# A four-layer network on one core: the second layer's input projections, two heads at a time, as seven half-size products a pair of blocks

## The reference, cut to what matters

```python
def odd_layer(x, norm_g, w_in, b_forget, w_out):
    hn = rmsnorm(x, norm_g)
    proj = hn @ w_in                      # (256, 2048) @ (2048, 4*2048 + 16)
    q, k, v, z, f_logit = jnp.split(proj, cuts, axis=-1)
    log_f = jax.nn.log_sigmoid((f_logit + b_forget).astype(jnp.float32))
    o = forgetting_attention(q, k, v, log_f)   # 16 heads of 128, causal
    o = o * jax.nn.silu(z)
    return x + o @ w_out
```

## Time and profile before

| | |
|---|---|
| median of three runs | 2799.68 us (2799.62 to 2801.92) |
| the profiled execution | 2801.85 us |
| its span, first to last instruction | 2800.0 us |
| mean granted TensorE clock, share of full speed | 0.997 |
| TensorE matmuls / weight loads busy | 2765.9 us (99%) / 2507.3 us (90%) |
| VectorE, ScalarE, GpSimd busy | 1165.1 (42%), 589.1 (21%), 216.8 us (8%) |
| read from HBM | 397.56 MB, 143 GB/s over the span |
| the 16 heads of the second layer | 554.66 to 1026.85 us |
| its output projection, 8 pairs | 1026.85 to 1126.94 us |

### The profile page before, as it was taken

The page is one execution under the profiler, slowest core; times in us unless marked ns, Lnnn a source line. Parts: engine busy times, 40 slices in busy tenths (PEclk is TensorE's granted clock), DMA queues, the critical chain, the costliest instruction groups (busy, mean ns, idle before and its releaser), DMA issues.

```text
span 2800.0 us, 45537 instructions
## 1 busy us (share of the span) xinstructions
PE 2765.9 (99%) x17268; PEld 2507.3 (90%) x17268; DVE 1165.1 (42%) x2805; ACT 589.1 (21%) x1321; POOL 216.8 (8%) x451
## 2 busy tenths in 40 slices
PE   8999999999999999999999999999999999999997
PEld 6888889999999999899999999888889999888897
DVE  6667665500001036544445541111113565444555
ACT  3221211111111112333333320111111012222211
POOL 0111110000000000222222210000000000000000
PEclk9999999999999999999999999999999999999999
DMA  6434433444343435333333326333332444444442
GB/s 233 143 129 148 140 115 135 153 167 148 136 149 136 149 135 194 122 120 123 132 133 123 134 97 228 134 120 120 120 136 79 177 165 162 163 155 150 150 166 105
DMA packets 63259, 400.50 MB, mean 143 GB/s; under 512 B 6705, under 2 KB 13377, under 8 KB 16865
## 3 DMA queue, kind: packets, MB, share of 16 engines
q1 hardware_dynamic: 62976, 397.58, 40.3%
q0 software_dynamic: 224, 2.11, 0.2%
HBM read 397.56 MB, written 2.11 MB: 143 GB/s over the span
## 4 chain that ended last, share of the span: by engine, by line
PE 97%; DVE 1%; issue 1%; ACT 1%; DMA 0%; POOLq 0%; DVEq 0%; ACTq 0%; SPq 0%
PE psum L502 55%; PE psum L555 18%; PE psum L511 12%; PE psum L774 2%; PE psum L946 1%; PE psum L622 1%; PE psum L718 1%; PE psum L629 1%; PE psum L876 1%; PE psum L645 1%; PE psum L655 1%; PE psum L838 1%; PE psum L531 1%; PE psum L541 0%; PE psum L874 0%
## 5 line engine op out<-in xcount | busy, mean ns | idle before, releaser
L502 PE MATMUL psum<-h,ring 128*128 128x256 f32 x7072 | 1572.8, 380 | 0.9 <-DVE h L1377 0.9
L502 PEld LDWEIGHTS psum<-h,ring 128*128 128x128 f32 x7072 | 1326.1, 190 | 186.9 <-issue 14.8
L511 PEld LDWEIGHTS psum<-ring,h 128*128 128x128 f32 x3072 | 350.3, 192 | 2.5 <-issue 0.2
L511 PE MATMUL psum<-ring,h 128*128 128x128 f32 x3072 | 350.9, 275 | 0.0
L555 PE MATMUL psum<-mix,ring 128*128 128x128 f32 x1768 | 210.5, 275 | 0.0
L555 PEld LDWEIGHTS psum<-mix,ring 128*128 128x128 f32 x1768 | 204.1, 192 | 0.2
L1531 DVE CUSTOM_DVE_ANT_0 score<-psum,near 128x128 f32<-128x128 f32 x96 | 29.3, 355 | 310.4 <-PE psum L622 305.9
L555 PE MATMUL psum<-h,ring 128*128 128x128 f32 x1024 | 120.0, 275 | 0.3 <-DVE near L1452 0.3
L555 PEld LDWEIGHTS psum<-h,ring 128*128 128x128 f32 x1024 | 117.1, 192 | 0.5 <-DVE near L1452 0.5
L1825 DVE COPY_PREDICATED small<-con,psum 128x256 f32<-128x256 uint32 x128 | 56.9, 445 | 81.6 <-PE psum L777 53.5
L1888 DVE CUSTOM_DVE_ANT_0 score_c<-psum,near_c 128x15 f32<-128x15 f32 x32 | 4.7, 174 | 155.8 <-PE psum L906 155.8
(11 more groups left out here) (394 smaller groups left out, 2760.8 us busy)
## 6 DMA issues: line engine op xcount, KB each, us to landing
ring<-w_out SPq DMA_DIRECT2D x80, 1024.0 KB, 5.2
ring<-w_odd SPq DMA_DIRECT2D x64, 1024.0 KB, 4.9
ring<-w_hgrn SPq DMA_DIRECT2D x64, 1024.0 KB, 4.9
ring<-w_even SPq DMA_DIRECT2D x48, 1024.0 KB, 4.9
ring<-w_nsa SPq DMA_DIRECT2D x48, 1024.0 KB, 4.9
ring<-w_rg SPq DMA_DIRECT2D x40, 1024.0 KB, 4.8
ring<-w_cmp_in SPq DMA_DIRECT2D x8, 1024.0 KB, 4.9
ring<-w_rgg SPq DMA_DIRECT2D x10, 512.0 KB, 5.6
```

Of the source, the lines that this page charges most:

```text
L502: mm = pe.matmul(dst[:, 0:T], tile(ph, n, k), h[:, k, :], start=k == 0, stop=k == KT - 1)
L511: mm = pe.matmul(dst[:, tt * P:(tt + 1) * P], h[:, k, tt * P:(tt + 1) * P], tile(ph, n, k), start=k == 0, stop=k == KT - 1)
```

## The change

The 16 heads become 8 turns of two heads (n and n + 8). A turn has four pairs of blocks (q, k, v, z, each of both heads), and each pair is done by `block_products` with its seven products; only q of the first turn stays direct: its two blocks are taken times the raw x and scaled by `rstd` afterwards. For v the tokens are the stationary operand (`tokens_out`). All pairs of the phase use one set of banks, 0 to 2 (`one_set`). The scores of both heads follow v's third product, the transposes z's third and fourth, and probabilities times values z's sixth. Sums of h are made once (`sums_odd`). The sums for the output projection are made head by head in each turn, and its first pair starts with seven of eight tiles (`late`).

The rows of the cumulated gates are fetched for two heads a turn by a GpSimd DMA, and the mask of both heads (four operations) is made when VectorE has read both of the turn before. The slots of the ring are dealt anew: the output projection of the first layer uses 0, 1, 2, 3 where it used 4, 0, 1, 2; the later phases follow. The block reads of ScalarE and the sums of VectorE are cut into functions (`first_reads`, `three_sums`, `fourth_sum`, `fifth_sum`) with the same operations. The scale of the scores moves from the copy of q into the exponential, and the cumulated gates are multiplied by sqrt(128) to match.

```diff
-        out1 = Phase(4, 14, four("w_out1", (4, 0, 1, 2)), (5, 6))
+        out1 = Phase(4, 14, four("w_out1", (0, 1, 2, 3)), (5, 6))
...
-        odd1 = Phase(HEADS, 4, [Load((3, 4, 0, 1)[n], tiles("w_odd1", n), SLOT, n + 1) for n in range(4)])
-        out2 = Phase(4, 14, four("w_out2", (2, 5, 3, 4)), (6, 7, 0))
+        odd1 = Phase(TWO_HEADS, 28, [Load(n % 4, tiles("w_odd1", n), SLOT, 7 * (n // 2) + 6 + n % 2) for n in range(8)],
+                     (5, 6))
+        out2 = Phase(4, 14, four("w_out2", (0, 1, 2, 3)), (5, 6))
...
+        fast_odd = Fast(odd1, tuple((2 * n, 2 * n + 1, None) for n in range(4)), 8, 8, True)
...
+                if first:
+                    for e in range(2):
+                        wait_load(pe, odd1, 0, e)
+                        for k in range(KT):
+                            mm = pe.matmul(bank[3 + e][:, 0:T], tile(odd1, e, k), raw[:, k, :], start=k == 0,
+                                           stop=k == KT - 1)
+                        mm.then_inc(used, 1 if e else 6)
+                    pe.wait_ge(h_ready, after(2 * KT))
+                else:
+                    block_products(fast_odd, i, 0, of_h, sums_odd, 12)
+                block_products(fast_odd, i, 1, of_h, sums_odd, 12)
+                block_products(fast_odd, i, 2, of_h, sums_odd, 12, None, (), ((3, scores),), 0, True)
+                block_products(fast_odd, i, 3, of_h, sums_odd, 12, None, (),
+                               ((3, lambda: turn(0)), (4, lambda: turn(1)), (6, mix_values)))
...
+            def masks(i):
+
+                causal = ccol("causal")
+                g.wait_ge(cum_in, 16 * (i + 1))
+                g.wait_ge(m_ready, after(2 * PAIRS + 2 * i))
+                for e in range(2):
+                    g.tensor_tensor(forget_mask[:, e, 0:P], causal[:, 0:P], cum_two[:, e, 0:P], ALU.add)\
+                        .then_inc(ck_ready, 1)
+                    g.tensor_tensor(forget_mask[:, e, P:384], causal[:, P:384], cum_two[:, e, :], ALU.add)\
+                        .then_inc(ck_ready, 1)
...
+            def two_heads(i, first, last):
+
+                base = 2 * PAIRS + 2 * i
+                if not first:
+                    three_sums(fast_odd, i, 0, q_two)
+                    three_forms(fast_odd, i, 1)
+                    fourth_sum(fast_odd, i, 0, q_two)
+                    fifth_sum(fast_odd, i, 0, q_two)
+                    fourth_form(fast_odd, i, 1)
+
+                three_sums(fast_odd, i, 1, k_two)
+                three_forms(fast_odd, i, 2)
+                fourth_sum(fast_odd, i, 1, k_two)
+                fifth_sum(fast_odd, i, 1, k_two)
+                fourth_form(fast_odd, i, 2)
+
+                three_sums(fast_odd, i, 2, v_two)
+                v.wait_ge(ck_ready, after(4 * i + 4))
+                for e in range(2):
+                    v.wait_ge(s_ready, after(base + e + 1))
+                    apart(v)
+                    masked_max(bank[3 + e], forget_mask[:, e, :], score[:, e, :],
+                               [stat[:, 0, t, e:e + 1] for t in range(2)])
+                    st.settle()
+                    v.tensor_scalar(nmax[:, e, :], stat[:, 0, :, e], -P ** -0.5, None, ALU.mult).then_inc(m_ready, 1)
+                three_forms(fast_odd, i, 3)
+                fourth_sum(fast_odd, i, 2, v_two)
+                for e in range(2):
+                    v.wait_ge(e_ready, after(base + e + 1))
+                    then(v.reciprocal(pinv[:, e, :], psums[:, e, :]))
+                    normalise(prob[:, e, :], [pinv[:, e, t:t + 1] for t in range(2)]).then_inc(p_ready, 1)
+                fifth_sum(fast_odd, i, 2, v_two)
+                fourth_form(fast_odd, i, 3)
+
+                three_sums(fast_odd, i, 3, z_two)
...
+                    three_forms(fast_odd, i + 1, 0)
+                fourth_sum(fast_odd, i, 3, z_two)
+                fifth_sum(fast_odd, i, 3, z_two)
...
+                    fourth_form(fast_odd, i + 1, 0)
                 v.wait_ge(z_tanh, after(i + 1))
-                v.scalar_tensor_tensor(gz[:, :], gate[:, :], 1.0, bank[1][:, 0:T], ALU.add, ALU.mult)\
-                    .then_inc(z_used, 1)
+                v.scalar_tensor_tensor(gate_two, gate_two, 1.0, z_two, ALU.add, ALU.mult).then_inc(z_used, 1)
                 v.wait_ge(z_used, after(i + 1))
                 v.wait_ge(o_ready, after(PAIRS + i + 1))
...
+                v.scalar_tensor_tensor(mixed, bank[7].rearrange("p (e t) -> p e t", e=2), 0.5, gate_two, ALU.mult,
+                                       ALU.mult).then_inc(o_used, 1)
+                v.wait_ge(o_used, after(PAIRS + i + 1))
+                sums([m[:, ds(i, 1), :] for m in sums2], mix[:, ds(16 + i, 1), :], mix[:, ds(24 + i, 1), :], 12 + 4 * i)
...
+            out_proj(fast2, 4, 0, range(16, 24), range(24, 32), sums2, 44, (7, o_used, after(PAIRS + TWO_HEADS), 40))
```

More of the change, by code:

```diff
@@ L565, in block_products @@
                     wait_load(pe, ph, i, f.pairs[q][2])
-                pe.wait_ge(first_read, after(2 * g - 2))
-                if late is None:
-                    run(first, lambda j: weights(f, q, 0, j), lambda j: mix[:, lo[j], early], True, begun)
+                pe.wait_ge(first_read, after(2 * g))
                 upto = kh if late is None else late[0]
[L570 to L573, removed]
+                run(1, first, block(0), lambda j: act(0, j, early), True, begun, upto)
                 for sem, value in banks_free:
@@ L577, in block_products @@
                 pe.wait_ge(sums_made, after(sums_needed - 2 if late is None else late[3]))
[L578 to L583, removed]
+                pe.wait_ge(later_read, after(5 * g - 1))
+                run(2, second, form(0), lambda j: sums[1][:, j], True, 0, upto)
@@ L584, in block_products @@
+                pe.wait_ge(later_read, after(5 * g))
+                run(3, third, form(1), lambda j: sums[0][:, j], True, 0, upto)
                 if late is not None:
-                    for n in f.pairs[1]:
-                        if n in (f.pairs[1][0], f.pairs[1][2]) and n is not None:
-                            wait_load(pe, ph, i, n)
+                    next_load, _, next_rest = f.pairs[1]
+                    wait_load(pe, ph, i, next_load)
+                    if next_rest is not None:
+                        wait_load(pe, ph, i, next_rest)
@@ L599, in block_products @@
                 pe.wait_ge(first_read, after(2 * g + 1))
-                run(first, lambda j: weights(f, q, 1, j), lambda j: mix[:, hi[j], early], False)
+                run(5, first, block(1), lambda j: act(1, j, early), False)
                 pe.wait_ge(forms_made, after(2 * g + 2))
                 pe.wait_ge(later_read, after(5 * g + 2))
-                run(second, form(2), lambda j: mix[:, hi[j], later], False)
+                run(6, second, form(2), lambda j: act(1, j, later), False)
@@ L1444, in fourth_form, with three_sums @@
                         st.mark(ins)
-            def combine(f, i, q, more, block, tail, between=None, scaled=False, final=False):
-                g = f.first + 2 * i + q
-                second, third = (bank[3 * q + n][:, 0:P] for n in (1, 2))
+            def three_sums(f, i, q, dst):
+                g = f.number(i, q)
+                second, third = (bank[f.bank(q) + n][:, 0:P] for n in (1, 2))
                 v.wait_ge(used, done(f.ph, i, 7 * q + 2))
                 v.wait_ge(first_read, after(2 * g + 1))
+                v.wait_ge(later_read, after(5 * g))
                 v.tensor_tensor(part_b, second, kept, ALU.add).then_inc(later_read, 1)
@@ L1725, in _ @@
             scale(raw)
+            v.wait_ge(h_ready, after(2 * KT))
+            sums(sums_odd, h[:, 0:8, :], h[:, 8:16, :], 8)
             v.wait_ge(used, done(forget, 0, 1))
```

330 lines of the change are left out of this document (183 added, 147 removed).

## The result

The changed kernel takes 2761.52 us, the median of four runs between 2761.49 and 2763.26; the kernel before took 2800.61 us in its four runs beside them (2799.62 to 2801.92). The ratio is 0.9862, with a 95% interval of 0.9845 to 0.9879. The forecast was 2761. The profiled execution took 2761.51 us, its span is 2759.8 us and its mean granted clock 0.998.

What follows compares the result with a forecast made beforehand. TensorE was taken as the bound, holding 97% of the last-ending chain. -44.1 + 4.9 + 0.7 = -38.5 us takes the profiled 2801.85 to 2763.4, median 2761 us; range 2753 to 2770.

Steps and rivals of the forecast that it cites:

- seven products, no wait: Second layer's heads: pairs at 12.51 us bring 472.2 down to 428.1 us, gaining 44.1 if TensorE never waits.
- v to z, seven turns: Between v's and z's pairs: GpSimd's masks slow VectorE, so TensorE waits 0.7 us a turn, 4.9 in all.
- end of a turn: VectorE's work after z's last unit delays the next pair's first read: 0 to 0.5 us, taken as 0.1 times 7.
- start of the layer: q's direct blocks, 13.8 us of TensorE, cover about 10 us of VectorE's work after the norm: no wait.
- second layer's output projection: The seven-tile start covers the last turn's sums, 6.3 us of TensorE against about 4.5: no wait.
- The floor of 428.1 us: Second layer's heads without waits: first turn 54.65 us plus seven turns of 53.35, against 472.2 before.
- The rival that narrow matmuls lose their price: Rival 3, every pair: half-width matmuls hide weight loads less; kernel 236 us longer, about 3036; chance 0.03.
- First output projection: First layer's output projection: forms start up to 4.5 us later, waiting for a load; cost taken as 0, at worst 2.
- The loads: Weight loads into freed slots and the cumulated gates' DMA arrive in time in the layer: no wait.
- Rival 1: VectorE keeps its slack and TensorE never waits: 2755.6 us; chance 0.25.
- Rival 2: GpSimd's masks cost VectorE more, 1.8 us a turn at v to z, or loads are late: 2766 to 2771; chance 0.18.

Runs made afterwards that it cites:

- run 7: Changed kernel with masks later, last sums later, second pair not started early, and first turn's first q block read before the three forms: 2756.32 us.
- run 1: Changed kernel, but GpSimd makes the next turn's masks only after the transposed probabilities are copied: 2761.34 us, heads 430.02 against 432.28.
- run 3: Changed kernel with the four output-projection sums moved from a turn's end behind q's fourth form in the next turn: 2759.79 us.
- run 4: Changed kernel with k's pair made direct in all eight turns, without forms or sums of its own: 2772.89 us.
- Run 5: Changed kernel, but the second pair of the second layer's output projection is not started early: 2760.94 us, output projection 100.83 against 101.70.
- run 6: Kernel before the change, with only the first output projection's loads in slots 0, 1, 2, 3: 2799.83 us beside 2799.66.
- run 2: Changed kernel with each turn's four GpSimd mask operations made twice, the extra ones into an unread part of the tile: 2768.84 us.

## Why the prediction was right, point by point

| term | forecast, us | measured, us | by |
|---|---|---|---|
| seven products, no wait | -44.1 | -44.4 | heads of run 7: 427.82 against 472.19 |
| v to z, seven turns | +4.9 | +2.3 | run 1; 0.36 in six turns, 0.07 in the first |
| end of a turn | +0.7 | +1.7 | run 3; 0.34 x 5 |
| start of the layer | 0 | +0.4 | run 7; 14.31 less 13.91 |
| second layer's output projection | 0 | +1.6 | stage table |
| sum | -38.5 | -38.4 | the stage table has -38.3 |

- **The products: right, and shown.** The floor of 428.1 us that the prediction works out from the earlier trace rows is reached by run 7 (427.82), and run 4 gives back 10.04 us for one pair in four where eight times 1.30 us, less 0.4 at the start, gives 10.0. The rival that narrow matmuls lose their price is out, and with it the spacing that the Trainium skill gives in "TensorE: Matmul & The Clock Gate", section "Back-to-back issue gap": 12.51 us over 112 matmuls against 13.82 over 64 is 0.52 a matmul for half the columns, where an estimate straight between the page's figures has 0.83.
- **v to z: the mechanism right, its size half.** The step that was mis-sized is "so VectorE loses about half the time in which GpSimd runs: 1.2 us", put in whole before the fourth sum. VectorE does lose 1.15 us, but only 0.67 of it there (0.25 and 0.41 in the forms); the other 0.48 is in a normalisation. So the fourth sum is done at 15.44 and not at 16.0 to 16.1, and TensorE waits 0.05 us for it instead of 0.5. The fifth sum is what it waits for, 0.31 us: the forecast has it at 17.9 or later, and it is done at 17.43, because the chain to it is 0.37 us shorter than counted (16.28 without masks, not 16.65). The Trainium skill, "SBUF — State Buffer", section "Who interferes with whom", has the form of it better than my scaling: the two exclude each other, the later waiting to the end of the earlier. The trace agrees for the forms (1.45, 1.70 and 1.43 us on GpSimd, 1.48 and 1.63 on VectorE), where GpSimd is the one that is held up most. What my estimate from it added, that two mask operations get in beside the forms and the others hold up the normalisations, is there too (1.03 instead of 0.55), but the 1 us a turn that it gave was further off than my own 0.7.
- **End of a turn: bound right, value low.** The step "I take 0.1" between 0 and 0.5; it is 0.34, and only five times. The read ends 0.15 us later than counted, the 0.15 from its end to TensorE was left out, and the loop's 0.45 was named but not priced; where it is missing there is no wait.
- **Start of the layer and output projection: "Nothing" twice, 0.4 and 1.6 us.** The first covered VectorE's work in sum, but not in order: what TensorE needs first stood behind what it needs later. The second counted the sums of the last turn (4.5 us under a cover of 6.3) and didn't ask what the early start does to the banks; the waits are for bank reads, not for sums. Run 5 shows it for 0.87 us; for the other 0.74 it is read from the trace.
- **First output projection: right.** Its forms start 3.44 us late and TensorE loses 0.1 us at most (run 6). (The prediction takes the end of VectorE's last gating from the first of its two operations; the second ends at 448.26, so the slack there was 2.0 us and not 2.4.)
- **The loads: right in the layer.** No wait of TensorE in the sixteen heads is put down to a DMA.

So the sum is as close as 0.2 us by luck: 2.6 us too much at v to z, 3.0 too little at three other places, and 0.3 more from the products. What was not luck is the first term, some fifteen times the size of any of these. Rival 1, "the cover holds", was wrong about all four waits, 6.0 us in all; run 7, which takes most of them away, comes to 2756.3, near its 2755.6. Rival 2 needed 1.8 us a turn at v to z, more than even twice the masks cost (1.04, run 2).

## What to carry to other kernels

A rate measured in one place of a kernel over hundreds of matmuls that wait for nothing carried here to another place of it, and gave most of the answer. What is left are the points where TensorE asks for a bank or an operand that stands in another engine's queue behind work that is needed later: walk through each of them, at the start, at the loop's turn and at the end of a phase too, by order and not by the sum of the work. Where VectorE and GpSimd add from SBUF at once, move GpSimd's part to a moment when nobody waits for VectorE: the two still collided in run 1, and yet one wait instruction took back 2.3 us.

## What the hardware showed that I had not expected

**A clock drop of some 2 us, that comes or doesn't.** Before the second layer there are two levels: profiled executions that reach it at 552.6 to 552.8 us and others at 554.6 to 555.0: those of before and of runs 1 and 2. The difference arises in the gated unit, behind a stretch in which TensorE is half idle. Windows of run 1, and the same of after (the columns as in the earlier trace rows, PEclk third from the right):

```profile
420.00:423.00 3.00, 1.30 (x7) 0.82 (x6) 2.14 (x6) 0.42 (x1) 0.00 (x0) 1.00 0.00 0
423.00:426.00 3.00, 2.87 (x9) 2.05 (x9) 1.61 (x4) 0.91 (x2) 0.00 (x0) 0.69 0.30 60
426.00:430.00 4.00, 4.00 (x17) 3.37 (x16) 0.00 (x0) 0.47 (x1) 0.00 (x0) 0.81 0.52 217
```

```profile
420.00:423.00 3.00, 1.31 (x6) 0.85 (x5) 1.83 (x6) 0.42 (x1) 0.00 (x0) 1.00 0.00 0
423.00:426.00 3.00, 2.87 (x13) 2.20 (x12) 1.61 (x4) 0.91 (x2) 0.00 (x0) 1.00 0.37 98
426.00:430.00 4.00, 4.00 (x20) 3.53 (x19) 0.85 (x2) 0.47 (x1) 0.00 (x0) 1.00 0.45 188
```

TensorE works 1.3 of the same 3 us in both, and then gets 0.69 and 0.81 of the full 2.4 GHz in the one and all of it in the other: part of these 7 us ran at the lower level of 1.2 GHz, and 7 us at 0.76 are 1.7 us less of full clock, about what is lost. Before's profile has 0.74 and 0.76 there, run 2's 0.81 and 0.72, and the other six have 1.00 twice. The runs' own times lie at two levels about as far apart, 2.3 and 1.8 us (2799.62 and 2801.92; 2761.49 and 2763.26); that it is the same drop there is likely, but no trace of those runs shows it. What decides whether it comes was not tried. For this case it means that the total of a single run cannot show 2 us, and that a stage can.
